# First feed-forward as seven half-size products per tile pair, with its down projection as a second phase; the last pair of both feed-forwards in another order

## What is computed

```
def swiglu(u, w_gate, w_up, w_down):
    return (jax.nn.silu(u @ w_gate) * (u @ w_up)) @ w_down

u = rmsnorm(h, ffn_norm[layer])
h = h + swiglu(u, ...)          # D_MODEL 1024, hidden width 2816
return h[:, N_META:]            # only after the last layer
```

## Time and profile before

| | |
|---|---|
| median of 3 runs | 3178.59 us (3176.72 to 3179.62) |
| the profiled execution, its own time | 3177.13 us |
| its span in the trace | 3175.3 us, 46997 instructions |
| mean granted TensorE clock | 0.992 |
| busy: PE, DVE, ACT, POOL | 97%, 56%, 29%, 42% of the span |
| first feed-forward in the trace | about 740 to 1503 us |
| second feed-forward | about 2455 to 3125 us |

### The profile page before, as it was taken

The page is one execution under the profiler, slowest core; times in us unless marked ns, Lnnn a source line. Parts: engine busy times, 40 slices in busy tenths (PEclk is TensorE's granted clock), DMA queues, the critical chain, the costliest instruction groups (busy, mean ns, idle before and its releaser), DMA issues.

```text
span 3175.3 us, 46997 instructions
## 1 busy us (share of the span) xinstructions
PE 3081.2 (97%) x18566; PEld 2785.7 (88%) x18566; DVE 1786.3 (56%) x2495; ACT 917.8 (29%) x1629; POOL 1341.3 (42%) x709
## 2 busy tenths in 40 slices
PE   8999999899999999999999999899999999999997
PEld 8999999899999999999999988566667788887886
DVE  6677777643333333334787852588888833334334
ACT  4466665621000000001112122233334533332101
POOL 4000000133444444444443444477674577775442
PEclk9999999999999999999999999999999999999998
DMA  3010000121111111111143423332323222223221
GB/s 122 25 36 32 22 25 16 42 88 41 47 46 45 41 46 46 46 46 42 68 139 90 131 87 113 111 121 89 118 89 118 65 84 80 80 84 126 99 86 67
DMA packets 133066, 230.27 MB, mean 73 GB/s; under 512 B 10006, under 2 KB 59414, under 8 KB 132886
## 3 DMA queue, kind: packets, MB, share of 16 engines
q1 hardware_dynamic: 93136, 180.21, 17.0%
q10 hardware_dynamic: 39749, 47.60, 4.5%
HBM read 180.77 MB, written 46.99 MB: 72 GB/s over the span
## 4 chain that ended last, share of the span: by engine, by line
PE 84%; DVE 7%; POOL 4%; issue 4%; ACT 1%; DMA 0%; DVEq 0%; ACTq 0%; POOLq 0%
PE PS L1066 77%; PE PS L1320 4%; PE PS L1305 2%; POOL Wlo L930 1%; POOL SQ L975 1%; POOL RMS L940 1%; DVE MX L2729 1%; PE PS L1618 1%; POOL SQ L970 1%; DVE GD L3111 0%; POOL STB L962 0%; DVE XW L3073 0%; PE PS L1766 0%; ACT PR L2049 0%; DVE KAP L3116 0%
## 5 line engine op out<-in xcount | busy, mean ns | idle before, releaser
L885 POOL TENSOR_TENSOR Whi<-Wraw,const 128x1024 fp32r<-128x1024 f32 x144 | 353.0, 2452 | 1472.3 <-PE PS L1066 925.1
L1066 PE MATMUL PS<-Uhi,Whi 128*128 128x352 f32 (+1 forms) x2276 | 566.5, 340 | 17.0 <-DVE Ulo L2521 13.9
L1066 PE MATMUL PS<-Ulo,Whi 128*128 128x352 f32 (+1 forms) x2276 | 562.2, 339 | 0.0
L1066 PE MATMUL PS<-Uhi,Wlo 128*128 128x352 f32 (+1 forms) x2276 | 561.1, 338 | 0.0
L1066 PEld LDWEIGHTS PS<-Uhi,Whi 128*128 128x128 f32 x2276 | 394.0, 189 | 39.5 <-issue 17.2
L1066 PEld LDWEIGHTS PS<-Uhi,Wlo 128*128 128x128 f32 x2276 | 397.1, 189 | 20.4
L1066 PEld LDWEIGHTS PS<-Ulo,Whi 128*128 128x128 f32 x2276 | 396.2, 188 | 20.6
L888 POOL TENSOR_TENSOR Wlo<-Wraw,Whi 128x1024 fp32r<-128x1024 f32 x144 | 394.6, 2741 | 11.3
L1066 PE MATMUL PS<-T,Whi 128*128 128x512 f32 x776 | 228.6, 395 | 3.3 <-DVE GATE L3322 1.6
L2862 DVE TENSOR_TENSOR H<-H,PS 128x1056 f32<-128x1056 f32 x88 | 110.3, 1254 | 130.7 <-PE PS L1066 130.6
L2978 DVE SCALAR_TENSOR_TENSOR YC<-XC,cols,YC 128x1052 f32<-128x1052 f32 (+1 forms) x96 | 180.8, 1884 | 3.4
(11 more groups left out here) (359 smaller groups left out, 6149.2 us busy)
## 6 DMA issues: line engine op xcount, KB each, us to landing
Wraw<-in_w SPq DMA_DIRECT2D x151, 512.0 KB, 3.2
Wraw<-in_w SPq DMA_DIRECT2D x152, 256.0 KB, 2.9
xt<-XTT ACTq DMA_DIRECT2D x20, 640.0 KB, 5.9
H<-in_x ACTq DMA_DIRECT2D x16, 528.0 KB, 8.4
zt<-ZB ACTq DMA_DIRECT2D x32, 256.0 KB, 2.1
X<-xt SPq DMA_DIRECT2D x8, 1024.0 KB
Z<-zt SPq DMA_DIRECT2D x32, 256.0 KB, 2.7
KFB<-keyf SPq DMA_DIRECT2D x15, 530.0 KB, 3.7
```

The lines of the kernel that those rows point to most:

```text
L885: pool.tensor_tensor(Whi[s][:], Wraw[s][:], ones.unsqueeze(1).broadcast_to([P, BLK, P]), ALU.mult)\
L1066: ins = pe.matmul(out, lhsT, rhs, start=start, stop=stop, skip_group_check=True)
```

## The change

The machinery of the second feed-forward becomes a class `Feed` and helpers that both feed-forwards use. What follows for the first one:

- Its four plain columns stay. The other 40 columns (2880 matmuls of 352) become 20 pairs of seven products; one of 528 columns is made as two matmuls of 264, in two banks: 4 blocks x 3 passes x 2 = 24 matmuls. All eight PSUM banks are used: 0, 1 or 2, 3 for the running sums of even and odd pairs, 4, 5 for product 2, and 6, 7 for products 5 and 3.
- The down projection moves behind all pairs: 5 groups of 4 tiles (36 matmuls of 352 for each output tile) and one of 2. The hidden tiles go through HBM. The last group is read into tiles of its own (`t[2]`).
- POOL makes 7 low factors and 4 sums for a pair, instead of splitting four units for two hidden tiles. ACT makes the high factors and the taps.
- The activations' sums are made by DVE and ACT beside the plain columns, from `H` that is complete by then. `b11_exact` (4 ACT copies of 528 columns) stands ahead of ACT's copy of the norm's factors to `RMS`, and eight differences of 528 columns on DVE between the norm's factors and the first plain gate.
- In the first pair of the first feed-forward, product 5 stands ahead of product 2, which waits for the group of the last plain up tile.
- Everything is written out; the hardware loops of the first feed-forward are gone.

For both: the last pair's order is now `(p,1) (p-1,4) (p-1,3) (p,6) (p,5) (p,7) (p,2) (p,4) (p,3)`, and DVE's order there is two `low_hidden`, quadrant 3, two `low_hidden`, quadrants 2, 0, 1.

```diff
-LAST_STEP = (0, 3, 4, 5, 1, 2, 6, 7)
...
-def product_order():
+def product_order(first):
     order = []
-    for p in range(PRODUCT_PAIRS):
-        if p == PRODUCT_PAIRS - 1:
-            order += [(p, 1), (p - 1, 4), (p, 6), (p - 1, 3), (p, 5), (p, 7), (p, 2)]
-            continue
+    for p in range(LAST_PAIR):
         order.append((p, 1))
         if p:
             order += [(p - 1, 4), (p - 1, 3)]
-        order += [(p, k) for k in (2, 6, 5, 7)]
-    return order + [(PRODUCT_PAIRS - 1, 4), (PRODUCT_PAIRS - 1, 3)]
+        order += [(p, k) for k in ((5, 2, 6, 7) if first and p == 0 else (2, 6, 5, 7))]
+    p = LAST_PAIR
+    return order + [(p, 1), (p - 1, 4), (p - 1, 3), (p, 6), (p, 5), (p, 7), (p, 2), (p, 4), (p, 3)]
...
+        f.hidden = [late if n == GROUPS_DOWN - 1 else (deep, flat)[n % 2] for n in range(GROUPS_DOWN)]
+        def bank(p, k):
+            if f.first:
+                b = {2: 4, 5: 6, 3: 6}.get(k, 2 * (p % 2))
+                return PS[:, b:b + 2, 0:L // 2]
+            b = {2: 6, 5: 7, 3: 7}.get(k, 3 + p % 2)
+            return PS[:, b:b + 1, :]
...
@@ PE: factor_product @@
                 for kt in range(KH):
-                    for j, (W, X) in enumerate(((OPHI, hi), (OPHI, lo), (OPLO, hi))):
-                        ins = mm(PS[:, bank, :], W[t % SLOTS][:, kt * P:(kt + 1) * P], X[:, kt, :],
+                    for j, (W, X) in enumerate(((f.ophi, hi), (f.ophi, lo), (f.oplo, hi))):
+                        for h in range(f.parts):
+                            ins = mm(bank[:, h, :], W[t % SLOTS][:, kt * P:(kt + 1) * P], X[:, kt, h * n:(h + 1) * n],
...
@@ PE: down_group @@
                     if n == 0 and m == 1:
-                        pe.wait_ge(quad_taken.sem, quad_taken.at(4 * PRODUCT_PAIRS))
+                        pe.wait_ge(f.quad_taken.sem, f.quad_taken.at(4 * PRODUCT_PAIRS))
+                    elif n == 0 and m == 0 and f.first:
+                        pe.wait_ge(f.quad_taken.sem, f.quad_taken.at(taken(LAST_PAIR, 2)))
...
-            with pe.Fori(0, F_STEPS - 2) as i, \
...
-                column(u0 + 2 * F_STEP)
-                down(u0 + 2 * F_STEP + 1)
-                for k in range(1, 2 * F_STEP):
-                    column(u0 + 2 * F_STEP + 2 + k)
...
+            for t in range(len(f.products)):
+                factor_product(t)
+            b[0] = 0
+            for n in range(GROUPS_DOWN):
+                down_group(n)
...
@@ ACT, first feed-forward @@
-        take_factors()
-        feed_forward(T)
+        b11_exact(f)
+        take_factors()
+        high_operand(f, 5, f.t1_made, KH)
+        plain_silu(f)
+        high_operand(f, 6, f.t2_made, KH)
+        high_operand(f, 7, f.t3_made, 1)
+        plain_silu(f)
+        for j in range(3):
+            high_factor(f, j)
+        high_operand(f, 4, f.t4_made, KH)
+        feed_products(f)
...
@@ DVE @@
+            ps = of if q != 3 else at if f.first else PS[:, 5:6, :]
...
+            for p in range(LAST_PAIR):
+                for q in (0, 3, 2, 1):
+                    take_quadrant(f, p, q)
+            low_hidden(f, 0, 0)
+            low_hidden(f, 0, 1)
+            take_quadrant(f, LAST_PAIR, 3)
+            low_hidden(f, 0, 2)
+            low_hidden(f, 0, 3)
+            for q in (2, 0, 1):
+                take_quadrant(f, LAST_PAIR, q)
...
+        f = feeds[0]
+        row_factor(f)
+        for k in range(KH):
+            first_difference(f, k)
+        for k in range(KH):
+            second_difference(f, k)
+        vec.wait_ge(rms_ready, c.want(rms_ready))
+        plain_gate(f, 0)
+        plain_up(f, 1)
+        third_difference(f)
+        plain_product(f, 1, 0)
+        low_operand(f, 5)
+        low_operand(f, 7)
+        plain_gate(f, 0)
+        fourth_difference(f)
+        low_operand(f, 6)
+        low_operand(f, 4)
+        plain_up(f, 1)
+        plain_product(f, 1, 1)
+        b = feed_quadrants(f, lambda m: low_u(m, "mix1"))
```

More of the change, by code:

```diff
@@ L174, in taken, with __init__, cut, half @@
 def taken(p, q):
-    return 4 * p + {0: 1, 3: 2, 2: 3, 1: 4}[q]
+    return 4 * p + (LAST_TAKEN if p == LAST_PAIR else TAKEN)[q]
+class Feed:
+    def __init__(self, k, u0, v0):
+        self.first, self.u0, self.v0, self.down = k == 0, u0, v0, v0 + PLAIN - 2
+        self.w = L if self.first else SEQ
+        self.n = NSEQ * self.w
+        self.gain = ("ffn0", "ffn1")[k]
+        self.parts = 2 if self.first else 1
+        self.products = product_order(self.first)
+        self.at = {x: t for t, x in enumerate(self.products)}
+        self.ready = {5: 1, 7: 2, 6: 3, 4: 4} if self.first else {6: 1, 5: 2, 7: 3, 4: 4}
+    def cut(self, ap):
+        return ap.rearrange("p (h n) -> p h n", h=self.parts)
+    def half(self, ap, s):
+        return ap[:, s * L + L - self.w:(s + 1) * L]
+    def halves(self, ap, k0, s):
+        return ap[:, k0:k0 + KH, s * L + L - self.w:(s + 1) * L]
+    def tile(self, ap):
+        return ap[:, 0:self.n]
+    def quarter(self, tiles, q):
+        return tiles[q // 2][:, q % 2 * self.w:(q % 2 + 1) * self.w]
 COLS = {}
@@ new lines, in plain_gate, with plain_up @@
+        def plain_gate(f, g):
+            vec.wait_ge(to_vector[g], c.want(to_vector[g]))
+            step(vec.tensor_tensor(f.rows(GATE[:]), f.group(g), f.rows(RMS[:]), ALU.mult)
+                 if f.first else
+                 vec.tensor_tensor(seqs(f.tile(GATE)), f.group(g), f.rows(RMS[:]), ALU.mult))
+            vec.sem_inc(grp_free[g], 1)
+            vec.sem_inc(gate_ready, 1)
+        def plain_up(f, g):
+            vec.wait_ge(to_vector[g], c.want(to_vector[g]))
+            step(vec.tensor_tensor(f.group(g), f.group(g), f.rows(RMS[:]), ALU.mult))
@@ new lines, in feed_quadrants @@
+        def feed_quadrants(f, after):
+            for p in range(LAST_PAIR):
[8 more added lines that the diff above has]
+                take_quadrant(f, LAST_PAIR, q)
+            b = 0
+            for n in range(GROUPS_DOWN - 1):
+                for m in range(KD):
+                    add_down(f, m, b, False)
+                    b ^= 1
+                    if 0 <= m - 3 < min(HG, F_TILES - HG * (n + 1)):
+                        low_hidden(f, n + 1, m - 3)
+                vec.sem_inc(f.down_added.sem, 1)
+            for m in range(KD if f.first else KD - 1):
+                add_down(f, m, b, True)
+                b ^= 1
+                if m and (f.first or m < KD - 2):
@@ L3413, in _ @@
[L3413 to L3424 removed]
+        f = feeds[1]
```

936 lines of the change are left out of this document (399 added, 537 removed).

## The result

| | before | after |
|---|---|---|
| median of the runs | 3179.11 us (3176.72 to 3181.80, 4 runs) | 3132.28 us (3128.38 to 3135.39, 4 runs) |
| profiled execution: own time, span | 3177.13, 3175.3 us | 3132.53, 3130.7 us |
| mean granted clock | 0.992 | 0.989 |

The ratio is 0.9853, 95% interval 0.9840 to 0.9865: 46.8 us faster. The forecast was 3126 us, with a range of 3117 to 3137.

A forecast was written before the change was run, and what follows sets the result against it. PE's stream of matmuls was taken as the bound. Products -55.3, opening +1.1, hand-overs +4.1 and -1.7 gave -51.8 us: 3125.3 us against the profiled execution, 3126 us as a median, range 3117 to 3137.

The forecast's parts named there:

- The product term: First feed-forward's products: 2880 matmuls of 352 columns (464.5 us) become 3360 of 264 (409.2 us), saving 55.3 us.
- first rival: First feed-forward's products: excess over streaming is fixed per matmul, 124.6 ns each, saving 45.8 us, total 3135.5 us; 7%.
- Steady pairs and down projection at nothing: First feed-forward: other engines' work stays covered by PE's matmuls in the pairs and down phase; cost 0.
- Slower than before through POOL: Pairs: POOL becomes the bound; the change loses from 23.1 us per pair, 3306 us at twice the instruction price; 2%.
- The opening: First feed-forward's start: PE waits 1.1 us at product 2 for DVE's late last plain tile; bounds 0 and 5 us.
- The hand-overs: Last pair to down phase: first feed-forward costs 4.1 us, second saves 1.7; waits of 3.0 and 2.7 us before product 3.
- second rival: Opening and hand-overs cost more, +13.5 us to 3139, and the clock may fall; 9%, at 3133 to 3141 us.
- the likeliest case: Whole kernel: the forecast itself, -51.8 us to 3126 us, own range 3117 to 3133, given 81%.
- the forecast's own sign: Hand-over: the forecast called itself wrong if the clock fell below 1.00 there.

The follow-up runs named there:

- the run with three more: Changed kernel with POOL making three of the seven low factors twice in 18 pairs of the first feed-forward: 3128.22 us, one execution.
- the two loads that were tried: Changed kernel with POOL making three, then all seven, low factors twice in 18 first feed-forward pairs: 3128.22 and 3201.45 us, one execution each.

## Why the forecast came out as it did

**The product term: right.** Forecast 409.2 us for 3360 matmuls at 121.8 ns; measured 121.9 ns, 409.7 us. The first rival (the excess fixed per matmul, 124.6 ns, 3135.5 us) is out on the same number, although the time alone, 3132.3, would have let it stand. The estimate by the Trainium skill (TensorE: Matmul & The Clock Gate, Back-to-back issue gap) stays 9 ns under the row, and the saving of the products measured is 54.8 us, not 51.7.

**Steady pairs and down projection at nothing: right.** No wait in either; POOL has 70.6 us busy in 100 [steady row above], 14.5 us per pair where 14.7 was forecast.

**Slower than before through POOL: the mechanism is real, and the kernel is far from it.** Its low factors take 1.33 us as before. POOL could have 25% more to do without a wait of PE, as the run with three more shows. The forecast's point, 23.1 us per pair, lies between the two loads that were tried and wasn't measured; by the measured gain it would be 20.5 + 46.8 / 20 = 22.8, an estimate.

**The opening: right in its first wait** (1.1 forecast, 1.2 measured, by the cause named, since moving the low parts removed it), and short of a second one of 0.7 behind POOL's low factor, which the forecast didn't look for: ACT makes the high part of operand 4, for which it waits 7.2 us on DVE's fourth differences, ahead of its next factors, so POOL's next low factor starts only at 799.0, behind 5.7 us idle.

**The hand-overs: their waits came out as forecast, and the step failed in the clock, which the sum put at nothing.** The forecast had waits of 3.0 and 2.7 us ahead of product 3, and 1.1 more at the first down tile. Measured are 3.4 and 3.6, and none at the tile. The low parts beside POOL were sized at 2.3 us and took 2.67, and behind quadrant 3 POOL was idle, so the next two took 1.21 and DVE caught up. By starts the wait costs 3.5 us in the first (4.1 forecast) and 3.7 in the second, against the 5.5 us that the four old waits cost: 1.8 gained, 1.7 forecast. What didn't is the clock. The forecast had it only in the second rival, at 9%, argued away by a row in which PE idles 4.5 us in pieces of 1.6; but its own working had put the pieces together into one wait, and with that the row no longer spoke of the case. It named one fall in the trace of the kernel before, at the earlier trace rows; that trace has more of them, also where PE waits, up to 4.0 us at a time (granted 0.83 over 2036 to 2076 us). In the profiled execution the clock fell in both hand-overs, so the rival's price was paid in part under the likeliest case. First one: 3.5 + 1.6 = 5.1 us in place of 4.1; second one: 3.7 + 2.8 = 6.5 against 5.5, 1.0 lost in place of 1.7 gained. In the run with the new order alone it is 5.4 against 5.5, nothing gained, and its time (0.9998) agrees without being fine enough to show it. The second rival's own sum is wrong as well: 3.9 + 3.9 + 3.7 is 11.5 us and 3137.5, not 13.5 and 3139.

**The sum by measured terms**, for the profiled execution and by distances of starts: -54.8 (products) + 2.4 (opening) + 5.1 + 1.0 (hand-overs) + 1.6 (the clock at the sums of squares) = -44.7, so 3132.4 against 3132.5 measured. That it fits so closely is in part luck: outside the stages that the change touches the two traces differ, too, by 1.4 us ahead of the first feed-forward, where the clock fell for longer (0.89 over 630 to 660 us, 0.94 before), and by differences of both signs behind it that nearly cancel this. The forecast had 3125.3. Of the 7.2 us between them about 6.0 are the clock at three places, 1.3 the opening, whose two waits cost 2.4 us by starts and not 1.1, and 0.5 the products; the waits of the hand-overs give back 0.7.

The mechanism was that of the likeliest case, with a part of the second rival in it, and by the forecast's own sign, a clock below 1.00 in the hand-over, that step was wrong. The time, 3132.3, is inside the forecast's own range (3117 to 3133), at its upper end. It owes this to the small size of the falls and not to a reason given for them: the same program in other executions took from 3128.38 to 3135.39 us.

## What to carry to other kernels

Where two streams of work meet, add up what the helping engine has to do behind the last point at which it is idle, and compare it with what the bound engine still has. If it is more, another order behind that point only moves the wait; what helped here was to start the work in the idle time before, at the cost of a short wait elsewhere. When waits are exchanged, write down the longest one beside their sum: four of 1.6 us at most kept the clock here, one of 2.6 to 3.6 mostly didn't, and each fall cost about as much as the exchange had saved. And a matmul's price at a new width is taken from a row of that width and weight load: proportion gave 264 columns to within 1 ns (121.0 for 121.9) and missed 132 by 50.

## What the runs showed of the hardware

- **The clock behind one long wait.** Of the fourteen hand-overs in these traces with one wait of 2.6 to 3.6 us eleven show a granted clock below 1.00 at its end or right behind it, down to 0.57 over 4 us; of seven whose longest wait is 0.8 to 1.6 us none does, though the sums reach 4.5 us. Both cases occur with the same program, so it is no certain thing. A fall cost about 1.6 us, the one in the second hand-over of the changed kernel 2.8. In the run with quadrant 3 first the wait stands at the second down tile and not ahead of product 3, and the clock fell there, too; the wait's length was never varied by itself.
- **Below some 240 columns a matmul's price is that of its weights.** At full clock 132 columns cost 111.7 ns, 264 cost 121.9, 352 cost 161.3: from 264 to 352 nearly in proportion to the columns, below that nearly flat. (The 240 is an estimate, where 161.3 / 352 ns per column meet 111.7 ns.) In the kernel before, matmuls of a single column show what sets the floor:

```profile
110.77 1.95 PE L1066 MATMUL PS<-const,SQ 128*106 128x1 f32 x20
...
753.51 2.29 PE L1066 MATMUL PS<-const,SS 128*128 128x1 f32 x20
```

  The next matmuls start at 112.57 and 755.66: 90 ns each with 106 columns of weights, 107.5 with 128. So one column costs nearly what 132 do, and the price goes with the columns of the weights. The Trainium skill (TensorE: Matmul & The Clock Gate, LDWEIGHTS (loading the stationary operand)) puts a load of 128 columns at P / 1.2, by an estimate from that page 107 ns; the trace agrees for one column, and with 132 columns it shows 111.7.
- **A stream of narrow matmuls lost the clock and didn't get it back.** With 132 columns PE went to the 1.2 GHz level behind a pause of 0.75 us, and from 820 to 2205 us it was busy without a break at a granted clock of 0.50. By an estimate from these prices that turned a loss of 341 us (6720 x 0.1117 - 409.7) into one of 995.
- **DVE beside POOL.** A low part of 1056 columns with both inputs in SBUF takes 1.21 us alone and 2.67 beside POOL's split; POOL's instruction of 2.4 us takes 3.3. The Trainium skill (SBUF — State Buffer, Who interferes with whom) calls the port pair that DVE shares with POOL an exclusive lock. By an estimate from that rule each low part would wait out up to a whole POOL instruction, 2.4 us; the rows show 1.46 us more. The same price falls on a quadrant that DVE finishes in SBUF: 1.58 and 2.79 us for 0.71.
